# Reordering loads, weight casts and gate rows in a fused mLSTM and SwiGLU block

## The reference

```python
mod = silu(c) @ ada_w + ada_b                      # six rows of 1024: sh1, sc1, g1, sh2, sc2, g2
h = rms_norm(x) * (1 + sc1) + sh1
q, k, v, o, gates = split(h @ w_in)                # 4 heads, q/k 128 wide, v/o 256 wide
gates = 15 * tanh((gates + b_if) / 15)             # log_i, f_pre ; log_f = log_sigmoid(f_pre)
hc = mlstm_chunkwise(q, k, v, log_i, log_f)        # running state C, n, m over chunks
y = (rms_norm(hc) * norm_w * sigmoid(o)) @ w_out
x = x + g1 * y
h = rms_norm(x) * (1 + sc2) + sh2
x = x + g2 * ((silu(h @ w_gate) * (h @ w_up)) @ w_down)     # 2816 hidden columns
out = rms_norm(x) * final_norm_w
```

## Time and profile before

| | us |
|---|---|
| median of three runs | 1132.93 (1132.18 to 1133.45) |
| the profiled execution | 1130.81 |
| its span, first to last instruction | 1129.0 |
| busy: TensorE (PE) / VectorE (DVE) / ScalarE (ACT) / GpSimd (POOL) | 1095.2 / 695.2 / 429.7 / 185.2 |
| PE not busy: 0 to 50 us | 14.9 |
| PE not busy: 1122 to 1129 us | 5.8 |
| PE not busy in the rest | 13.1 |

### The profile page before, as it was taken

The page is one execution under the profiler, slowest core; times in us unless marked ns, Lnnn a source line. Parts: engine busy times, 40 slices in busy tenths (PEclk is TensorE's granted clock), DMA queues, the critical chain, the costliest instruction groups (busy, mean ns, idle before and its releaser), DMA issues.

```text
span 1129.0 us, 15219 instructions
## 1 busy us (share of the span) xinstructions
PE 1095.2 (97%) x5517; PEld 928.3 (82%) x5517; DVE 695.2 (62%) x1172; ACT 429.7 (38%) x767; POOL 185.2 (16%) x151
## 2 busy tenths in 40 slices
PE   5999999999999998999999999999999998999997
PEld 4798888888787898988888888888888886888886
DVE  5856745455455737666676767566756456744676
ACT  6863221321322413363333333333333316344444
POOL 5632312212324434730000000000000000000000
PEclk9999999999999999999999999999999999999999
DMA  9415533422432423112645354525452889566553
GB/s 368 158 63 187 157 97 95 147 94 75 154 112 56 169 94 131 76 38 75 215 161 194 110 179 162 193 93 197 149 187 95 295 300 354 187 197 194 190 165 149
DMA packets 87194, 178.17 MB, mean 158 GB/s; under 512 B 8120, under 2 KB 31288, under 8 KB 86096
## 3 DMA queue, kind: packets, MB, share of 16 engines
q1 hardware_dynamic: 86416, 175.07, 46.2%
q0 software_dynamic: 704, 2.13, 0.6%
HBM read 137.02 MB, written 40.16 MB: 157 GB/s over the span
## 4 chain that ended last, share of the span: by engine, by line
PE 56%; DVE 1%; DMA 1%; ACT 0%; issue 0%; SPq 0%; DVEq 0%; ACTq 0%
PE OP L2080 26%; PE O L2080 15%; PE ST L2080 5%; PE AD L2080 5%; PE DC L2080 5%; DMA dF<-w_units 1%; PE ST L1862 0%; PE O L1862 0%; DVE hL L1242 0%; DVE x L1707 0%; DVE tL L1242 0%; DVE x L1714 0%; DVE dL L1616 0%; ACT junk L1026 0%; ACT dH L1074 0%
## 5 line engine op out<-in xcount | busy, mean ns | idle before, releaser
L1833 PE MATMUL OP<-wH,hH 128*128 128x256 f32 (+1 forms) x448 | 150.9, 337 | 0.0
L1833 PE MATMUL OP<-wH,hL 128*128 128x256 f32 (+1 forms) x448 | 147.3, 329 | 0.0
L1833 PE MATMUL OP<-wL,hH 128*128 128x256 f32 (+1 forms) x448 | 147.2, 329 | 0.0
L1616 DVE TENSOR_TENSOR dL<-dF,dH 128x1024 fp32r<-128x1024 f32 x77 | 92.5, 1222 | 73.5 <-ACT dH L1074 72.6
L1074 ACT CAST dH<-dF 128x1024 fp32r<-128x1024 f32 x77 | 79.6, 1053 | 95.6 <-DMA dF<-w_units 34.8
L2080 PE MATMUL OP<-tH,wsH 128*128 128x512 f32 x264 | 102.9, 390 | 0.0
L2080 PE MATMUL OP<-tH,wsL 128*128 128x512 f32 x264 | 102.7, 389 | 0.0
L2080 PE MATMUL OP<-tL,wsH 128*128 128x512 f32 x264 | 102.7, 389 | 0.0
L1833 PEld LDWEIGHTS OP<-wH,hL 128*128 128x128 f32 x448 | 84.9, 190 | 7.9
L1833 PEld LDWEIGHTS OP<-wH,hH 128*128 128x128 f32 x448 | 85.0, 190 | 7.1 <-DVE hL L1345 0.3
L1833 PEld LDWEIGHTS OP<-wL,hH 128*128 128x128 f32 x448 | 85.1, 190 | 6.8
(11 more groups left out here) (311 smaller groups left out, 2694.9 us busy)
## 6 DMA issues: line engine op xcount, KB each, us to landing
raw<-w_units SPq DMA_DIRECT2D x76, 512.0 KB, 4.7
dF<-act_mid SPq DMA_DIRECT2D x77, 256.0 KB, 2.6
ada<-ada_rest SPq DMA_DIRECT2D x64, 256.0 KB, 3.0
wst<-w_units SPq DMA_DIRECT2D x44, 256.0 KB, 5.0
down_mid<-wst SPq DMA_DIRECT2D x22, 512.0 KB, 3.2
dF<-down_mid SPq DMA_DIRECT2D x44, 256.0 KB, 2.9
dF<-w_units SPq DMA_DIRECT2D x33, 256.0 KB, 5.9
ada<-ada_first SPq DMA_DIRECT2D x8, 1024.0 KB, 10.1
```

Of the source, the lines that this page charges most:

```text
L1616: nc.vector.tensor_tensor(dL[g][:], dF[g][:], dH[g][:].bitcast(F32), ALU.subtract).then_inc(d_L, 1)
L1833: ins = nc.tensor.matmul(out_ap, lhs[a], rhs[b], start=(n == 0 and i == 0), stop=(last and i == 2))
```

## The change

In the first head ScalarE's exponent of row SI and the cast of unit 2 move from tiles 2 and 3 to tile 4, and TensorE's row transposes move from after tile 4 to after tile 5. The casts of unit 3 move from chunk 0 (both) to chunks 1 and 5, their low halves from chunks 0 and 1 to chunks 2 and 6, and the load of the second piece of unit 4 from ada item 8 to item 14. In the last head GpSimd scales the second piece of U_OUT+1 at chunk 5 instead of 6 and applies head norms 0 and 1 at chunk 6 and 2 at chunk 7; norm 2 leaves VectorE. ScalarE casts U_OUT+1 around og_high(0), VectorE makes its low half right after og_low(1), and the steps of units U_OUT+2, U_OUT+3 move forward in the same way. SP issues the load of U_OUT+2 after two of the four x2 transfers. At the end of the up product SP issues save_act, the loads of down steps 10 and 11 and the two saves first, then fw and step 12, and the eight x loads each behind one of the loads of steps 13 to 20.

```diff
--- before.py
+++ after.py
@@ -432,8 +432,8 @@
                 load_unit(h * 3 + 3)
                 ada_bias(h, 0, first)
                 for i in range(2, 16):
-                    if i in (6, 8):
-                        load_unit(h * 3 + 4, (i // 2 - 3,))
+                    if i in ((6, 14) if first else (6, 8)):
+                        load_unit(h * 3 + 4, (int(i > 6),))
                     ada_item(h, i, first)
                     if i == 12:
                         ada_bias(h, 1, first)
@@ -451,7 +451,8 @@
             for i in range(4):
                 sp.dma_start(x2[:, 2 * i:2 * i + 2, :],
                              x[2 * i:2 * i + 2].rearrange("t p n -> p t n")).then_inc(x2_in[i], 16)
-            load_unit(U_OUT + 2)
+                if i == 1:
+                    load_unit(U_OUT + 2)
             mod_store(2 * NH - 1)
             load_unit(U_OUT + 3)
 
@@ -562,18 +563,18 @@
             load_step(9)
             save_chunk(NF - 2)
             load_chunk(NF - 1)
-            for t in range(4):
-                load_x(t, (end, 7))
-            for t in range(4, NT):
-                load_x(t, (end, 3))
             save_act(NG - 1)
+            load_step(10)
+            save_sums(NG - 1)
+            load_step(NG)
+            save_chunk(NF - 1)
             sp.wait_ge(c_L, 7 * NF)
             sp.dma_start(fw[:], final_w.to_broadcast([P, D])).then_inc(fw_in, 16)
-            load_step(10)
-            save_sums(NG - 1)
-            save_chunk(NF - 1)
-            for s in range(NG, STEPS):
+            for s in range(NG + 1, STEPS):
                 load_step(s)
+                t = s - (NG + 2)
+                if 0 <= t < NT:
+                    load_x(t, (end, 7 if t < 4 else 3))
             for t in range(4):
                 sp.wait_ge(f_out, t + 1)
                 sp.dma_start(out[t], x3[t][:]).then_inc(out_done, 16)
@@ -701,17 +702,19 @@
                             pool.wait_ge(o_mm, h * NT)
                         nc.gpsimd.tensor_tensor(qs[:, c % 2, :], qT[:, c * P:(c + 1) * P],
                                                 sI[:, c * P:(c + 1) * P], ALU.mult).then_inc(qs_ok, 1)
-                    if last and c == 7:
+                    if last and c == 6:
                         head_norm(0)
                         head_norm(1)
+                    if last and c == 7:
+                        head_norm(2)
                     if 1 <= c:
 
                         pool.wait_ge(hc_ok, h * NT + c)
                         pool.wait_ge(gate_ok, h * NT + c)
                         nc.gpsimd.tensor_tensor(hg[:, c - 1, h * DV:(h + 1) * DV], hc[:, (c - 1) % 2, :],
                                                 gate[:, (c - 1) % 2, :], ALU.mult).then_inc(hg_ok, 1)
-                    if last and c in (4, 6):
-                        scale_unit(U_OUT + 1, (c // 2 - 2,))
+                    if last and c in (4, 5):
+                        scale_unit(U_OUT + 1, (c - 4,))
 
             for h in range(NH):
                 head(h, h == 0, h == NH - 1)
@@ -929,10 +932,9 @@
                         nc.scalar.copy(va[:, t, 0:DV], OP[t % 2][:, 0:DV]).then_inc(v_ev, 1)
                     if t < 4:
                         evac_qk(0, t)
-                    if t == 2:
+                    if t == 4:
                         act.wait_ge(g_dve, 6)
                         nc.scalar.activation(row(SI), row(SI), ACT.Exp).then_inc(g_act, 1)
-                    if t == 3:
                         split_H(2, 2, (gates_mm, 2))
                     if t == 6:
                         act.wait_ge(rT_cp, 2)
@@ -944,8 +946,8 @@
                         decay(0, c + 1)
                     act.wait_ge(op_mm, c + 1)
                     gate_tanh(0, c, OP[c % 2][:, 0:DV])
-                    if c == 0:
-                        split_H(3, 0, (qk_mm, 4))
+                    if c in (1, 5):
+                        split_H(3, 0, (qk_mm, 4), (c // 4,))
                     if c:
                         squares(0, c - 1)
 
@@ -982,15 +984,16 @@
             first_head()
             for h in range(1, NH):
                 head(h)
+            split_H(U_OUT + 1, 1, (v_mm, NH * NT), (0,), 2)
             og_high(0)
             squares(NH - 1, NT - 2)
+            split_H(U_OUT + 1, 1, (v_mm, NH * NT), (1,), 2)
             squares(NH - 1, NT - 1)
             head_root(1)
             for t in range(1, NT):
                 og_high(t)
                 if t == 4:
-                    split_H(U_OUT + 1, 1, (v_mm, NH * NT), scaled=2)
-            split_H(U_OUT + 2, 2, (v_mm, NH * NT), scaled=3)
+                    split_H(U_OUT + 2, 2, (v_mm, NH * NT), scaled=3)
             split_H(U_OUT + 3, 0, (y_mm, NT), scaled=4)
 
             def up_cast(n, q):
@@ -1438,8 +1441,8 @@
                     if c:
                         divide(0, c - 1)
                         gating(0, c - 1)
-                    if c < 2:
-                        split_L(3, 0, (c,))
+                    if c in (2, 6):
+                        split_L(3, 0, (c // 4,))
                     if c == 5:
                         mod_row(0)
                     ada_item(0, 2 * c)
@@ -1488,8 +1491,8 @@
                 nc.vector.tensor_tensor(x2[:, t, cols], x2[:, t, cols], Y_BANKS[n % 4][:, 0:DV],
                                         ALU.add).then_inc(y_ev, 1)
 
-            head_norm(2)
             og_low(1)
+            split_L(U_OUT + 1, 1)
             mod_row(2 * NH - 1)
             head_rstd(1)
             y_tile(0)
@@ -1499,13 +1502,11 @@
                 if t % 2 == 0 and t + 2 < NT:
                     head_norm(t + 2)
                 if t == 5:
-                    split_L(U_OUT + 1, 1)
+                    split_L(U_OUT + 2, 2)
             y_tile(NT - 1)
             for n in range(NT, 2 * NT):
                 y_tile(n)
                 if n == NT + 1:
-                    split_L(U_OUT + 2, 2)
-                if n == NT + 6:
                     split_L(U_OUT + 3, 0)
             dve.wait_ge(sc2_in, 16)
             nc.vector.tensor_scalar(sc2[:], sc2[:], 1.0, None, ALU.add).then_inc(sc2_ok, 1)
@@ -1943,10 +1944,10 @@
 
             def out_transposes(t):
 
-                if t and t % 2 == 0:
-                    pe.wait_ge(og_n[0], t // 2)
+                if t in (4, 6):
+                    pe.wait_ge(og_n[0], t // 2 - 1)
                 else:
-                    pe.wait_ge(og_n[1], (t + 1) // 2 + 1)
+                    pe.wait_ge(og_n[1], t + 1 if t < 3 else (t + 5) // 2)
                 for j in range(2):
 
                     if t == 0:
@@ -2000,7 +2001,7 @@
                         pe.wait_ge(g_sum, t + 1)
                     project(OP[t % 2][:, 0:DV], h_tile(t),
                             lambda k: tuple(w[:, k, :] for w in wv)).then_inc(v_mm, 1)
-                    if t == 4:
+                    if t == 5:
                         row_transposes()
                 pe.wait_ge(qk_ev, 4)
                 pe.wait_ge(v_one, 1)
```

## The result

The changed kernel takes 1117.69 us at the median (1117.15 to 1117.69) against 1132.93 (1130.64 to 1133.45) of the kernel before beside it: a ratio of 0.9867 [0.9853, 0.9881], 15.2 us. The range of the changed kernel is that of three executions; two more ran at a mean granted clock of 0.85 and 0.75, took 1220.67 and 1373.32 us, and are left out. One more comparison on another chip gave 1117.94 against 1133.73, 0.9863 [0.9848, 0.9877].

The account below looks back on a forecast made before the run. TensorE, busy for 1095.2 of 1129.0 us, was taken to bound the kernel. Terms of 6.25 + 1.05 + 1.3 + 0.5 + 3.4 = 12.5 us off the 1132.93 median gave 1120.4 us, range 1118.0 to 1125.0.

Parts of the forecast that it names:

- down steps: Start of the down product: store ahead of x loads removes waits of 0.77 and 3.78 and the low clock, 6.25 us.
- gate rows: First head: one more tile ahead of the row transposes covers TensorE's wait for VectorE, 1.05 us gained.
- casts of unit 3: First head: moving casts and low halves removes two TensorE waits of 0.66 us at chunks 1 and 2, 1.3 gained.
- out transposes: End of last head: the 2.00 us wait for head norm 0 goes, but only 0.5 us arrives by y tile 2.
- rows of x: After the output product: the 2.95 us wait for GpSimd's shift and 0.45 of the 0.97 go, 3.4 us together.
- The rival by which the rows bind elsewhere: At the rows of x, the wait removed at row 0 returns at row 3 or 5; 3.4 lost, 1123.8 us; chance 0.17.
- The one on GpSimd and VectorE: GpSimd holds VectorE up: 1 us lost in the first head, 1.9 before y tile 2; 1123.3 us; chance 0.13.
- The last line of the sum: Whole kernel: the median's 2.1 us over the profiled execution stays, so 1132.93 - 12.5 = 1120.4 us; chance 0.60.
- The low end of the range: Whole kernel: 1118.0 us, the better case less 0.4 of scatter.
- the better case of the terms alone: Out transposes and rows of x: the whole 2.00 and 0.97 us arrive, 14.5 gained, 1118.4 us; chance 0.05.

Follow-up runs that it names:

- no_a: The changed kernel with SP's down-step order of the kernel before; 1124.11 us, and 1122.93 us when run again on another chip.
- norms_late: The changed kernel with GpSimd's head norms 0 and 1 back at chunk 7 and norm 2 behind them; 1117.27 us.
- scale_late: The changed kernel with the scaling of U_OUT+1's second piece back at chunk 6; 1118.35 us.
- u3_late: The changed kernel with the low half of U_OUT+3 back after y tile 14 instead of 9; 1123.16 us.
- spread_low: The changed kernel with U_OUT+1's two low halves made apart, U_OUT+2's pieces likewise, the second loaded behind all four x2 transfers; 1117.42 us.
- a_only_again: The same kernel as a_only, run once more on another occasion; 1127.26 us.
- a_only: The kernel before with only SP's new order at the end of the up product; 1127.07 us, ratio 0.9948.
- c_only: The kernel before with only the first head's edits; 1130.12 us, ratio 0.9971.
- after_again: The changed kernel, unedited, run again on the chip of fill; 1117.94 us.
- fill: no_a with 14 throwaway matmuls on TensorE ahead of the wait for down step 11; 1122.31 us.

## Why the prediction was right or wrong

| term | told | ledger |
|---|---|---|
| down steps | 6.25 | 6.31 |
| gate rows | 1.05 | 1.13 |
| casts of unit 3 | 1.3 | 1.85 |
| out transposes | 0.5 | 0.71 |
| rows of x | 3.4 | 3.50 |
| start of the kernel | 0 | -0.39 |
| sum, profiled executions | 12.5 | 13.1 |

- **Down steps: right**, by their mechanism as well. no_a gives 6.4 in the median. The store took 3.1 us until step 10's load was issued where I took 4.5, and step 11 was ready 8.7 us before its turn (920.88 for 929.59) where I had told 6.5; no x load was late. The low clock was in this term, since the profiled execution of before showed it.
- **Gate rows: right.** The row transposes run at 81.71 with no wait, and the exponent behind ScalarE's table load cost TensorE nothing.
- **Casts of unit 3: right in kind, 0.55 short.** Both waits (0.66 and 0.67 us) are gone, and no new one stands between 88 and 132 us. The other half us is what a stop costs besides its idle time: 0.92 us each by the rows above, and 2 x 0.92 = 1.84 of the 1.85. The prediction priced each stop at its idle time alone; the 1.13 for 1.05 at the gate rows, the 2.17 for 2.00 and the 3.11 for 2.95 are above it too.
- **Out transposes: right in sum, with the reason half wrong.** Of its own, y tile 1 gained 2.17 + 0.02 - 0.74 = 1.45 us (1.4 told), and by y tile 2 half of that was spent again. The new waits were 0.77 and 0.47 where 0.5 and 0.9 were told. That the 2.00 us go because of the norms is only one of two sufficient causes (norms_late, scale_late).
- **Rows of x: right.** 2.95 and 0.32 of the 0.97 us went (told: 2.95 and 0.45), the 2.95 only with the edit that was named (u3_late). The rival by which the rows bind elsewhere is out: nothing came back at row 3 or 5. The one on GpSimd and VectorE is out too: before y tile 2 they kept apart (369.42, 372.13 and 375.30), and in the first head they overlap, but VectorE starts first and its two low halves take 1.22 us each (at 99.32 and 118.69). spread_low shows that the effect itself is real.
- **The last line of the sum: wrong.** This is the step that failed. The profiled execution of 1130.81 was forecast to become 1118.3 and became 1117.69, 0.6 off, which are the small misses above, most of them the price of a stop. Then the text said: "The median lies 2.1 us over the profiled execution, so the forecast is 1132.93 - 12.5". That carries an offset of before over to after, as if it were noise that any kernel has. The offset is gone in after, whose profiled execution is its median. In its place the runs show clock lost behind the waits of 2.00 and 2.95 us in executions other than the profiled one (2.80, 1.27 and 2.86 us in three traces, and 1.6 us less in the median with these waits filled), and these waits are what the change removes; 0.39 of the 2.1 us can be the early start of before's profiled execution. Before's own executions with the mean clock of the profiled one lie at 1130.7, those with a lower one (0.996 to 0.994) at 1133.1. The low clock was priced only behind the wait of 3.78, where the profile happened to show it; at the other two it was put at nothing. The low end of the range held none of it: it came from the better case of the terms alone.

## What to carry to other kernels

Price a wait of TensorE of 2 us or more at its length and, on top, at the clock that it may cost, whether or not the profiled execution shows a low clock behind it; here that was 1.1 to 1.7 us each at the two places of the output product, and 1.5 to 2.7 behind the down stall, in the executions that had it. Add 0.1 to 0.25 us for the stop itself. If the median of a kernel lies above its profiled execution and the executions spread, ask which waits could make that offset before carrying it over to the changed kernel; the mean granted clock of each execution sorts them. Do not add up parts by the spans of single executions: here 3.0 + 2.4 - 1.0 = 4.4 of 13.1 us, since each execution lost its clock at other places. The medians gave 5.7 + 4.7 + 2.6 = 13.0 of 15.2, and with intervals of 1.2 to 1.6 us on each part the missing 2.2 are not clear of noise. The first stretches, up to the out transposes, agreed to 0.07 us wherever a part left them alone.

## What the runs showed of the hardware

- A wait of TensorE of 2.00 us at the same place of the same instructions left the clock at 1.00 in before and a_only_again and took it to 0.58 over the next 4 us in a_only and to 0.57 in c_only (366 to 370). That it depends on the execution and not on the wait's length alone I had not expected.
- Throwaway matmuls in the wait kept the clock at 1.00 in all three places tried. The spread was 0.45 us against 3.1 in the partner beside it and 1.9 against 4.7; but no_a, unfilled, spread over 1.1 us in five runs on another chip, so that they steady the kernel is likely and not shown. It is worth something only where the wait itself can't be removed: after_again, without the waits, is 4.4 us faster than fill beside it.
- Early in the kernel, from 16 to 28 us, the clock was 0.60 to 0.63 in eight of the sixteen traces and 1.00 in the other eight. The first value tile started between 63.96 and 65.33 us in the eight with the low clock and between 63.95 and 65.00 in the others: no relation. The DMA share of that window is 1.02 or 1.03 in all sixteen; TensorE isn't what is waited for there.
